# Expert gate and up products of a mixture-of-experts layer: taken in turns, block by block, in place of all gate blocks first

## What is computed

```python
def expert_block(args):
    xb, e = args
    return (jax.nn.silu(xb @ w_gate[e]) * (xb @ w_up[e])) @ w_down[e]
```

## Time and profile before

| | us |
|---|---|
| median of 3 runs | 1817.06 (1816.35 to 1817.12) |
| span of the profiled execution, first to last instruction | 1814.6 |
| TensorE busy | 1726.1 |
| VectorE, ScalarE, GpSimd busy | 588.1, 510.6, 275.0 |
| expert loop on TensorE, first gate product to last down product | 989.8 to 1771.1 |

### The profile page before, as it was taken

How to read it: one execution, slowest core, us unless ns; L and a number is a source line. 1 busy time by engine, 2 the same in 40 slices (tenths; PEclk the granted TensorE clock), 3 DMA queues, 4 the chain that set the end, 5 groups by cost and what they waited for, 6 DMA issues and landing times.

```text
span 1814.6 us, 30930 instructions
## 1 busy us (share of the span) xinstructions
PE 1726.1 (95%) x11376; PEld 1285.8 (71%) x11377; DVE 588.1 (32%) x1562; ACT 510.6 (28%) x1303; POOL 275.0 (15%) x344
## 2 busy tenths in 40 slices
PE   6899999999999999999978999999999999999990
PEld 5667676776767767677647778878878888878880
DVE  1444445534455334553356111111111111111114
ACT  1444333443344433444423111111111111111113
POOL 0001011010110101101011212222222222222132
PEclk9999999999999999999989999999999999999995
DMA  9411011100111001111024889889999899999998
GB/s 352 109 59 36 24 58 58 58 35 23 58 58 56 36 23 58 58 52 41 23 89 150 299 288 330 282 290 320 338 308 323 278 338 311 309 320 318 305 302 338
DMA packets 130536, 322.42 MB, mean 178 GB/s; under 512 B 10744, under 2 KB 18953, under 8 KB 130500
## 3 DMA queue, kind: packets, MB, share of 16 engines
q1 hardware_dynamic: 113988, 278.71, 43.6%
q0 software_dynamic: 15648, 43.11, 9.2%
q10 hardware_dynamic: 864, 0.10, 0.0%
HBM read 274.86 MB, written 47.19 MB: 177 GB/s over the span
## 4 chain that ended last, share of the span: by engine, by line
PE 91%; DVE 2%; DMA 2%; ACT 2%; issue 2%; POOL 0%; ACTq 0%; DVEq 0%; POOLq 0%; SPq 0%
PE bank L299 15%; PE bank L293 14%; PE bank L1209 13%; PE bank L1220 13%; PE bank L1245 12%; PE bank L321 11%; PE bank L288 3%; PE bank L1177 2%; PE bank L1234 1%; PE bank L467 1%; PE bank L373 1%; PE bank L957 1%; PE bank L416 1%; PE bank L397 1%; ACT fjunk L1386 1%
## 5 line engine op out<-in xcount | busy, mean ns | idle before, releaser
L299 PE MATMUL bank<-uT,w_in_sb 128*128 128x128 f32 x2304 | 276.9, 279 | 2.3 <-DVE uT L643 2.3
L299 PEld LDWEIGHTS bank<-uT,w_in_sb 128*128 128x128 f32 x2304 | 267.8, 194 | 11.1 <-issue 8.9
L1209 PEld LDWEIGHTS bank<-xT,wts 128*128 128x128 f32 x2048 | 248.7, 191 | 25.0 <-issue 20.9
L293 PE MATMUL bank<-w_in_sb,uT 128*128 128x512 f32 (+1 forms) x768 | 261.5, 494 | 0.0
L1209 PE MATMUL bank<-xT,wts 128*128 128x128 f32 (+2 forms) x2048 | 253.0, 283 | 6.0 <-issue 5.1
L1220 PE MATMUL bank<-xT,wts 128*128 128x128 f32 (+2 forms) x2048 | 247.9, 282 | 0.0
L1220 PEld LDWEIGHTS bank<-xT,wts 128*128 128x128 f32 x2048 | 245.0, 191 | 0.0
L1245 PE MATMUL bank<-wts,hT 128*128 128x512 f32 x512 | 231.7, 595 | 0.0
L321 PE MATMUL bank<-w_out_sb,mixT 128*128 128x512 f32 x512 | 222.7, 593 | 1.5 <-ACT mixT L517 0.8
L293 PEld LDWEIGHTS bank<-w_in_sb,uT 128*128 128x128 f32 x768 | 127.1, 190 | 110.2 <-issue 110.2
L1300 DVE TENSOR_TENSOR hT<-bank,sg 128x160 f32<-128x160 f32 x128 | 41.6, 325 | 443.8 <-PE bank L1220 443.8
(11 more groups left out here) (246 smaller groups left out, 1703.3 us busy)
## 6 DMA issues: line engine op xcount, KB each, us to landing
wts<-w_gate_in SPq DMA_DIRECT2D x32, 2048.0 KB, 10.8
wts<-w_up_in SPq DMA_DIRECT2D x32, 2048.0 KB, 9.5
wts<-w_down_in SPq DMA_DIRECT2D x32, 2048.0 KB
x_sb<-x_in SPq DMA_DIRECT2D x17, 512.0 KB, 3.6
xT_in<-x_t_in SPq DMA_DIRECT2D x17, 512.0 KB, 4.8
w_in_sb<-w_in_in SPq DMA_DIRECT2D x4, 2048.0 KB, 12.1
h_sb<-x_in SPq DMA_DIRECT2D x16, 512.0 KB, 3.2
h_dram<-h_sb SPq DMA_DIRECT2D x16, 512.0 KB, 2.9
```

Of the source, the lines that this page charges most:

```text
L293: m = pe.matmul(bk[name][:, col:col + hi - lo], uT[:, k, :], w_in[:, k, lo:hi], start=k == 0, stop=k == KD - 1)
L299: m = pe.matmul(bk[name][0:hi - lo, col:col + P], w_in[:, k, lo:hi], uT[:, k, :], start=k == 0, stop=k == KD - 1)
L1209: m = pe.matmul(G[m_ % 2][:, 0:w], wg[:, k, m_ * P:(m_ + 1) * P], xT[:, k, 0:w], start=k == 0, stop=k == KD - 1)
```

## The change

`pe_gate` and `pe_up` now make one block each and take its number `m_`; `pe_chunk` calls them in turns: gate block 0, up block 0, gate block 1, up block 1, and so on. Products, semaphores and their counts stay what they were, and so does every other engine's program. The overflow turns use the same functions.

```diff
-    def pe_gate(pe, pre, n, w):
-        for m_ in range(KF):
-            if m_ == 0:
-                wait(pe, sem(f"{pre}w_gate_loaded"), 16 * (n + 1))
...
-            m.then_inc(sem(pre + "g_done"), 1)
+    def pe_gate(pe, pre, n, w, m_):
+        if m_ == 0:
+            wait(pe, sem(f"{pre}w_gate_loaded"), 16 * (n + 1))
...
+        elif m_ >= 2:
+            after(pe, pre, "sg_ready", 4 * n + m_ - 1)
...
+        m.then_inc(sem(pre + "g_done"), 1)
+
+    def pe_up(pe, pre, n, w, m_):
+        if m_ == 0:
+            wait(pe, sem(f"{pre}w_up_loaded"), 16 * (n + 1))
+            after(pe, pre, "h_ready", 4 * n)
+        elif m_ >= 2:
+            after(pe, pre, "h_ready", 4 * n + m_ - 1)
...
+        m.then_inc(sem(pre + "u_done"), 1)
+
+    def pe_chunk(pe, pre, n, w, next_x):
...
-        pe_gate(pe, pre, n, w)
-        pe_up(pe, pre, n, w)
+            pe_gate(pe, pre, n, w, m_)
+            pe_up(pe, pre, n, w, m_)
```

More of the change, by code:

```diff
@@ L1212, in pe_up @@
-    def pe_up(pe, pre, n, w):
-        for m_ in range(KF):
[L1214 to L1223, removed]
-        pe_gate(pe, pre, n, w)
-        pe_up(pe, pre, n, w)
+    def pe_gate(pe, pre, n, w, m_):
+        if m_ == 0:
+            wait(pe, sem(f"{pre}w_gate_loaded"), 16 * (n + 1))
+            after(pe, pre, "yA_taken", 2 * n - 1)
+            if pre == "m_":
+                after(pe, pre, "xT_ready", 3 * n + (3 if w > P else 1))
+            else:
+                after(pe, pre, "yD_taken", 2 * n - 1)
+                after(pe, pre, "xT_ready", 4 * n + 2)
+        elif m_ >= 2:
+            after(pe, pre, "sg_ready", 4 * n + m_ - 1)
+        for k in range(KD):
+            if m_ == 0 and k == 4 and pre == "o_":
+                after(pe, pre, "xT_ready", 4 * n + 4)
+            elif m_ == 0 and k == 4 and w == P:
+                after(pe, pre, "xT_ready", 3 * n + 2)
+            m = pe.matmul(G[m_ % 2][:, 0:w], wg[:, k, m_ * P:(m_ + 1) * P], xT[:, k, 0:w], start=k == 0, stop=k == KD - 1)
+        m.then_inc(sem(pre + "g_done"), 1)
@@ new lines, in pe_up @@
+    def pe_up(pe, pre, n, w, m_):
[4 more added lines that the diff above has]
+            after(pe, pre, "h_ready", 4 * n + m_ - 1)
+        for k in range(KD):
+            m = pe.matmul(U[m_ % 2][:, 0:w], wu[:, k, m_ * P:(m_ + 1) * P], xT[:, k, 0:w], start=k == 0, stop=k == KD - 1)
+        m.then_inc(sem(pre + "u_done"), 1)
+    def pe_chunk(pe, pre, n, w, next_x):
+        for m_ in range(KF):
+            pe_gate(pe, pre, n, w, m_)
+            pe_up(pe, pre, n, w, m_)
```

## The result

| | before | changed |
|---|---|---|
| median, us | 1817.09 (4 runs) | 1883.49 (4 runs, 1880.91 to 1889.96) |
| ratio to before, 95% interval | | 1.0367 [1.0353, 1.0381] |
| profiled execution: time / span / granted clock | span 1814.6, clock 0.983 | 1889.96 / 1887.9 / 0.972 |

A forecast was written before the change was run, and what follows sets the result against it. TensorE was taken as the bound, busy 1726.1 of 1814.6 us. New wait +37.9, `sg` waits -2.7 and clock +11 make +46; with the 2.5 us offset of the median, 1863 us, range 1838 to 1905.

The forecast's parts named there:

- The new wait: TensorE ahead of the first up block: gate and up loads need 14.1 us, 128-wide turns give 11.55; +37.9 us in all.
- The rate: Up load lands behind the gate load by its own bytes: 2.097 MB at 388 GB/s, 5.4 us.
- TensorE's clock: Behind the new pauses of 2.2 to 2.6 us, half of 13 long ones drop the clock: +11 us, ends 0 and 22.
- ScalarE's `sg` wait: Gate block 2's 16 waits for the first `sg` go, as an up block now stands between: -2.7 us.
- The DMA engines look free by then.: At the gate load's issue, 13 to 16 us into the turn, scatter, gather and down load are done; so 14.1 us.
- The clock holds: Rival: all as forecast, but without clock drops behind TensorE's pauses; 1852 us, chance 0.2.
- The pair is quicker: Rival: gate and up loads need 13.1 us, 1.45 us wait behind 128-wide turns, no clock drops; 1833 us, chance 0.13.
- The pair is slower: Rival: gate and up loads meet other transfers or a lower rate; 0.9 us more gives 1897 us, chance 0.19.
- Not slower: Rival: both loads land within 11.55 us, so no new wait and no `sg` waits; 1814 us, chance 0.05.

The follow-up runs named there:

- The filler run: Changed kernel with 4 extra, overwritten products put into the first up bank ahead of the wait for the up load: 1875.98 us, ratio 1.0314.
- the run with one address: Changed kernel with every load of the loop taking the weights of expert 12, at a constant address: 1873.92 us, ratio 1.0311.
- the order with the last gate block earlier: Changed kernel with only the last gate block one block earlier (G0 U0 G1 U1 G2 G3 U2 U3): 1849.04 us, ratio 1.0177.
- the order with the first up block later: Changed kernel with only the first up block one block later (G0 G1 U0 U1 G2 U2 G3 U3): 1833.69 us, ratio 1.0078.

## Why the prediction was right, and where its sizes were off

The sign, the place and the mechanism were right: idle time ahead of the first up block, ended by the up load, with the gate load landing in 8.3 us before its turn and the clock at half behind some pauses. The measured 1883.49 lies in the range, 20 us above the forecast.

*The new wait.* Forecast +37.9 us, measured +50. The wait behind a typical 128-wide turn, 2.54 us, is the 2.55 that was worked out. Three things were mis-sized. From the first issue the forecast gave the pair 13.6 us. It took that at best, but 14.2 on average behind 128-wide turns and up to 15.4 in turns 0, 1 and 5 (the first turn is 0). Behind wide turns I put 2.3 us in all; there were 7, with 1.97 and 1.19 behind turns 6 and 7. And of the 6.1 us of idle time that I took off as cover for the load, 1 us stands ahead of the first turn, where it covers nothing; only 3.9 us stood in turns with a wait for the up load. Lengthening the pair by little counts in every turn, as the short up load showed the other way round.

*The rate.* The landing of the up load 5.4 us behind the gate load's bears out the 388 GB/s, against the 358 of the Trainium skill (DMA: Bandwidth & Descriptors, "Where 436 GB/s comes from").

*TensorE's clock.* Forecast +11 us, half of the 13 long pauses; measured 22 to 24.5 in the profiled run and, by the granted clocks of the other three, 12 to 18. The 13 had no working behind it, and the half was a choice. The trace has 18 pauses of 1.97 to 3.2 us ahead of up products, and 13 low stretches behind them, where I expected some 6. At 47.8 us in all, half of which is lost, they make 24 us, about the upper end of 22. The filler run and the run with six eighths of the up load show that it is the pause that costs this. Even one of 1.97 us in dense work was followed by a drop, here in the changed kernel:

```profile
1185.84 1.51 PE L1218 MATMUL bank<-xT,wts 128*128 128x144 f32 x8 [1.97 <-DMA wts<-w_up_in]
```

```profile
1187.00:1190.00 3.00, 3.00 (x14) 3.00 (x14) 0.33 (x1) 0.00 (x0) 1.85 (x4) 0.50 1.00 287
```

So the rule of the Trainium skill (TensorE: Matmul & The Clock Gate, "Why this matters for your kernels"), which warns of longer gaps only, would have been wrong by this whole term. The length of the pause alone doesn't decide, though. The shortest pause in any run's loop with a low stretch behind it was 1.87 us (in the run with one address), and the longest without one was 3.23 us (in the order with the last gate block earlier):

```profile
1374.04 2.05 PE L1218 MATMUL bank<-xT,wts 128*128 128x128 f32 x16 [3.23 <-DMA wts<-w_up_in]
```

```profile
1374.00:1380.00 6.00, 5.96 (x53) 5.97 (x54) 0.57 (x2) 0.30 (x1) 2.57 (x4) 1.00 1.06 303
```

In the run with six eighths of the up load, whose longest pause in the loop was 1.57 us, there was none.

*ScalarE's `sg` wait.* Forecast -2.7 us, and the waits are gone. The run with hardly any up load came out 8.2 us under the kernel before, so the gain was larger: a 128-wide turn takes 22.25 us in place of 22.50, 4.5 us over 18 turns, and 0.07 comes off each 144-wide one. The rest wasn't taken apart; part of it may be the lighter traffic.

*"The DMA engines look free by then."* True for the changed kernel. It is not true one block earlier, as the order with the gate block moved showed: 11 us into a turn the gather is still moving. "Only the sum of the two distances counts" was my expectation there, and it failed for this reason.

*The rivals.* "The clock holds" (1852) is excluded by the 0.52 rows. "The pair is quicker" is excluded by the landings. "The pair is slower" with 0.9 us more gave 1897, and the truth lies about halfway to it. "Not slower" was what the short up load made, by taking away 7/8 of the transfer.

## What to carry to other kernels

Where one buffer of weights is reloaded behind its last use, the order of use is also the order of prefetch. Count for each buffer the time from its last use to its next first use, and compare it with the landing of everything that is queued with it, not of one load. An order that releases the first buffer early and needs the second late (two gate blocks, an up block, two gate blocks, three up blocks) gets the gain of taking turns without its price. And in this kernel 13 of 18 pauses of some 2 us or more on TensorE were followed by a stretch at half clock, which cost some 1.8 us each on top of the pause (24 us in all).

## What the runs showed of the hardware that was not expected

The clock fell to its lower level behind pauses as short as 1.87 us, but not behind each pause of that length or longer (one of 3.23 us stayed without), and not equally often from run to run. Of the changed kernel's spread of 9 us much is that; but it is not the only source of spread, as the order with the first up block later spread over 11 us at a granted clock of 0.983 to 0.984. Putting products that nobody needs into each pause, 0.9 us of them in a 128-wide turn, made the kernel 7.5 us faster. Two 2 MiB loads that were queued together landed 13.6 us after the first issue at best, but 15.2 where 0.64 MB of gather moved among them. And SP issued a load 0.16 us sooner when its address was a constant.
